# Branch A's output tiles: two gates taken from the buffers, and weights issued ahead of gates in SP's queue

## What is computed

```python
z = h @ p['w_in']
za, zb, zg = jnp.split(z, [A_COLS, A_COLS + B_COLS], axis=-1)
y_a, new_rwkv = _rwkv7_branch(za_mix, s_rwkv, p)
y_b, new_ret = _retention_branch(zb, s_ret, pos)
gates = jax.nn.sigmoid(zg.astype(jnp.float32)).reshape(bsz, t, 2, D_MODEL)
merged = (gates[:, :, 0] * (y_a.astype(h.dtype) @ p['w_branch_a'])
          + gates[:, :, 1] * (y_b.astype(h.dtype) @ p['w_branch_b']))
out = merged.astype(h.dtype) @ p['w_out']
```

## Time and profile before

| | |
|---|---|
| median of 3 runs | 4482.52 us (4481.86 to 4484.15) |
| profiled execution | 4492.62 us, span 4490.8 us |
| mean granted clock of TensorE | 0.958 of full speed |
| busy: PE, DVE, ACT, POOL | 94%, 44%, 31%, 6% of the span |
| DMA | 448.88 MB, mean 100 GB/s |
| loads of queries and keys, of values, of a head | 1280 KB each |
| weights of a branch A tile, a gate, a spilled tile | 512, 320, 320 KB |
| retention head 0 beside `ba`, first to last eviction | layer 0: 1252.3 to 1356.1 us, layer 1: 3498.1 to 3603.0 us |

### The profile page before, as it was taken

One profiled execution on the slowest core, in us unless ns is written; L12 is line 12 of the kernel. 1 busy time (PEld: TensorE's weight loads), 2 busy tenths in 40 slices (PEclk: granted clock), 3 DMA queues, 4 the chain that ended last, 5 costly groups with the idle time before them and its releaser, 6 DMA issues.

```text
span 4490.8 us, 87125 instructions
## 1 busy us (share of the span) xinstructions
PE 4208.0 (94%) x37680; PEld 3751.5 (84%) x37680; DVE 1955.1 (44%) x3032; ACT 1389.2 (31%) x2168; POOL 288.9 (6%) x464
## 2 busy tenths in 40 slices
PE   6999999999989987999989999999999899889997
PEld 5888899888866676999978888998888666789996
DVE  2444444434245543433354444444442455554444
ACT  3333333324223222322233333333242232232222
POOL 1000000000001111000100000000000011000000
PEclk7999999999989997999979999999999899989998
DMA  5122212212355565243421222122123465412221
GB/s 174 60 61 69 61 61 62 63 58 70 107 165 205 181 196 173 85 125 118 129 71 60 61 68 62 58 64 65 59 70 107 162 208 181 157 34 75 74 75 64
DMA packets 477320, 448.88 MB, mean 100 GB/s; under 512 B 18846, under 2 KB 409048, under 8 KB 476064
## 3 DMA queue, kind: packets, MB, share of 16 engines
q1 hardware_dynamic: 417712, 253.05, 18.6%
q0 software_dynamic: 41840, 157.01, 10.8%
q10 hardware_dynamic: 17408, 33.56, 2.0%
HBM read 345.79 MB, written 97.76 MB: 99 GB/s over the span
## 4 chain that ended last, share of the span: by engine, by line
PE 85%; DVE 7%; DMA 3%; ACT 3%; issue 2%; POOL 0%; ACTq 0%; DVEq 0%; SPq 0%; POOLq 0%
PE ps L731 83%; DVE scr L1915 2%; PE ps L735 1%; DMA w_raw<-in_w_branch_a_dram 1%; ACT scr L1372 1%; DMA scr<-in_ada_w_dram 1%; ACT w_hi L1385 1%; DVE acc L1915 1%; DVE h_lo L1915 1%; DVE w_lo L1928 1%; DVE scr L1917 1%; DVE lw L1915 1%; DMA w_raw<-in_w_out_dram 0%; ACT scr L1522 0%; DMA w_raw<-in_w_branch_b_dram 0%
## 5 line engine op out<-in xcount | busy, mean ns | idle before, releaser
L731 PE MATMUL ps<-h_hi,w_hi 128*128 128x320 f32 x4544 | 1105.1, 325 | 96.8 <-DVEq L1923 55.4
L731 PE MATMUL ps<-h_lo,w_hi 128*128 128x320 f32 x4544 | 1042.6, 311 | 0.0
L731 PE MATMUL ps<-h_hi,w_lo 128*128 128x320 f32 x4544 | 1041.6, 311 | 0.0
L731 PEld LDWEIGHTS ps<-h_hi,w_hi 128*128 128x128 f32 x4544 | 749.1, 190 | 185.1 <-issue 159.8
L731 PE MATMUL ps<-scr 64*64 64x64 f32 (+10 forms) x13248 | 809.5, 250 | 14.3 <-ACTq L1504 14.1
L731 PEld LDWEIGHTS ps<-scr 64*64 64x64 f32 (+4 forms) x13248 | 590.8, 141 | 212.6 <-issue 182.1
L731 PEld LDWEIGHTS ps<-h_lo,w_hi 128*128 128x128 f32 x4544 | 767.4, 190 | 0.0
L731 PEld LDWEIGHTS ps<-h_hi,w_lo 128*128 128x128 f32 x4544 | 766.3, 189 | 0.0
L1385 ACT ACTIVATE w_hi<-w_raw 128x1024 fp32r<-128x1024 f32 (+1 forms) x468 | 410.6, 878 | 797.7 <-PE ps L731 595.4
L1928 DVE TENSOR_TENSOR w_lo<-w_raw,w_hi 128x1024 fp32r<-128x1024 f32 (+1 forms) x468 | 469.4, 1003 | 364.0 <-ACT w_hi L1385 345.0
L1372 ACT ACTIVATE scr<-ps 128x512 f32<-128x512 f32 (+8 forms) x724 | 343.8, 475 | 780.4 <-PE ps L731 558.6
(11 more groups left out here) (151 smaller groups left out, 2946.2 us busy)
## 6 DMA issues: line engine op xcount, KB each, us to landing
w_raw<-in_w_in_dram SPq DMA_DIRECT2D x180, 512.0 KB, 3.8
scratch_z<-scr SPq DMA_DIRECT2D x128, 320.0 KB, 2.2
scr<-in_ada_w_dram POOLq DMA_DIRECT2D x40, 1024.0 KB, 6.1
scr<-in_state_ret_dram POOLq DMA_DIRECT2D x64, 512.0 KB, 4.8
out_dram<-scr ACTq DMA_DIRECT2D x64, 512.0 KB, 3.0
w_raw<-in_w_ffn_up_dram SPq DMA_DIRECT2D x64, 512.0 KB, 4.1
w_raw<-in_w_ffn_down_dram SPq DMA_DIRECT2D x128, 256.0 KB, 2.7
scr<-scratch_z POOLq DMA_DIRECT2D x24, 1280.0 KB, 9.0
```

Source lines behind the costliest of these rows:

```text
L731: return pe.matmul(out, lhsT, rhs, start=start, stop=stop, skip_group_check=True)
```

## The change

Spilled tiles are now 62 a layer (`STORED`): the last two, gates 6 and 7, stay in `ZT`. Branch A's tile i computes output tile (i + 6) % 8, so tiles 0 and 1 multiply with these two gates; their weights and their place in `ACC` move along. POOL's wait for `z_out` stands for 62 tiles and its two loads are gone, with the semaphore `gate_first`. Gates 0 to 5 are loaded by SP for tiles 2 to 7. In SP's queue the weights of tile i come first, behind the wait for the slot alone, and behind them the gate of tile i-1 with its wait for the eviction of tile i-3; at the last tile the gates of tiles 6 and 7 both.

```diff
+STORED = SPILLED - 2
             if name == "ba":
-                return ba_v[l, i]
+                return ba_v[l, (i + KD - 2) % KD]
...
                     if not isinstance(g, int) or g >= 2:
                         sp.wait_ge(lo_done, g - 1)
-                    if name == "ba" and i >= 2:
-                        sp.wait_ge(psum_read_v, freed(g - 1, "v"))
-                        sp.dma_start(ZT[:, i % 2], scratch["z"][GATE0 + i]).then_inc(gate_in[i % 2], 16)
                     sp.dma_start(WR[:, s, 0:kt], weight_of(l, name, i)).then_inc(w_in[s], 16)
+                    if name == "ba":
+                        for t in (i - 1, i) if i == KD - 1 else (i - 1,):
+                            if t >= 2:
+                                sp.wait_ge(psum_read_v, freed(START[l, "ba"] + t - 1, "v"))
+                                sp.dma_start(ZT[:, t % 2], scratch["z"][GATE0 + t - 2]).then_inc(gate_in[t % 2], 16)
...
-                        if kind == "own":
-                            spilled[g] = (l * SPILLED + i, i)
+                        if kind == "own" and i < STORED:
+                            spilled[g] = (i, i)
...
                 for i in range(2):
-                    po.wait_ge(z_out[i], 16 * (SPILLED // 2) * (l + 1))
-                    po.dma_start(ZT[:, i], scratch["z"][GATE0 + i]).then_inc(gate_first[i], 16)
+                    po.wait_ge(z_out[i], 16 * (STORED // 2) * (l + 1))
...
-                            f = l * SPILLED + o
+                            f = l * STORED + o
...
                             if i < 2:
-                                ve.wait_ge(gate_first[i], 16 * (l + 1))
+                                ve.wait_ge(psum_read_a, freed(START[l, "ba"], "a"))
                             else:
                                 ve.wait_ge(gate_in[i % 2], 16 * ((KD // 2 - 1) * l + i // 2))
-                            ve.tensor_tensor(halves(ACC[:, i]), two_banks(0), halves(ZT[:, i % 2]), MUL_).then_inc(psum_read_v, 1)
+                            ve.tensor_tensor(halves(ACC[:, (i + KD - 2) % KD]), two_banks(0), halves(ZT[:, i % 2]), MUL_).then_inc(psum_read_v, 1)
```

More of the change, by code:

```diff
@@ L402, in build @@
         stage_sem = {n: sem(n) for n in STAGES}
-        gate_first = [sem("gate_first0"), sem("gate_first1")]
         ya_hi, ya_lo, gate_in = sem("ya_hi"), sem("ya_lo"), [sem("gate_in0"), sem("gate_in1")]
```

## The result

| | before | after |
|---|---|---|
| median | 4483.34 us (4 runs, 4481.86 to 4484.44) | 4447.35 us (4 runs, 4442.24 to 4456.60) |
| profiled execution | 4492.62 us, span 4490.8 | 4442.60 us, span 4440.8 |
| ACT's waits for w_branch_a | 157.8 us, 12 waits | none |
| ba0 to ba7, layer 0 and 1 | 103.82 and 104.90 us | 88.54 and 87.21 us |

The ratio after to before is 0.9924, with a 95% interval of 0.9908 to 0.9941: 34 us of 4483, between 26 and 41. The forecast was 4446.7 us, a gain of 35.8.

A forecast was written before the change was run, and what follows sets the result against it. PE was taken as the bound, stalled behind ACT's waits for late branch A weights. Gains of 17.4 us in layer 0 and 18.4 in layer 1, other parts zero: 4482.5 - 35.8 = 4446.7 us, range 4438 to 4462.

The forecast's parts named there:

- The bound and the waits: Branch A beside head 0: ACT's twelve waits for weights, 157.8 us, all go; ba6's weights get about 23.5 us of lead.
- The control: Head 1's intervals, plus 3.53 us for 24 more matmuls, size head 0's: sum 75.6 us, gains 17.4 and 18.4 us.
- Interval 5 to 6: Head 0, between evictions of ba5 and ba6: forecast 13.4 us, between 12.75 and 16.28.
- The rival that DVE holds the tail: DVE's rotary pieces keep interval 5 to 6 at 18.25 and 17.39 us: gain falls 4.9 + 4.0, 4455.6 us; 12 in 100.
- Idle time and clock: Check on head 0's PE: 8.0 us idle plus 5.1 us clock, 13.1 a layer, 26 us as low end of the gain.
- Gates from the buffers: Gates 6 and 7 kept in ZT, POOL's states earlier: cost and gain zero, bound 0 to 1 us per layer.
- The gates' new place: Gates 2 to 7 behind weights in SP's queue, wanted 23 us or more later: zero; bb0's weights 0.5 us at most.
- The slower rival: A late gate, at gates 6 and 7, holds up eviction and PE: 4507 us if each lands at 28 us; 2 in 100.
- The time: Whole kernel: gain 35.8 us from 4482.5, giving 4446.7 us; 80 in 100 for 4440 to 4453.

The follow-up runs named there:

- run 7: Changed kernel with weights of branch A tile i held until the eviction of tile i-3: 4450.22 us, ratio 0.9936.
- run 11: Changed kernel with no DVE rotary piece between evictions 5 and 6 of a head, the first at point y1: 4445.58 us, ratio 0.9916.
- run 4: Changed kernel with the next head's first rotary piece on DVE moved ahead to point y1, later pieces one place forward: 4445.36 us, ratio 0.9908.
- Run 2: Changed kernel with SP's old queue put back, so only the new order of the tiles remains: 4469.46 us, ratio 0.9967.
- Run 6: Kernel before with POOL loading head 0's first three states and gates ahead of its two waits for spills: 4471.75 us, ratio 0.9982.
- run 1: Kernel before with SP's queue alone changed, branch A weights ahead of gates: 4451.87 us, ratio 0.9926.
- run 3: Changed kernel again, unaltered, for a second profile: 4449.29 us, ratio 0.9923.
- run 10: Changed kernel with each gate waiting for one eviction more, bb0's first weights behind them: 4459.68 us, ratio 0.9945.
- run 12: Kernel before again, unaltered, for a second profile: 4482.96 us in one execution.
- run 5: Changed kernel with weights of tile i waiting again for the eviction of tile i-2, gates still behind: 4467.56 us, ratio 0.9969.

## Why the prediction was right, point by point

**The bound and the waits.** Right. Twelve waits were forecast to go and twelve went. The lead is ample, though shorter than the 23.5 us of the prediction: ba6's weights left 20.2 us ahead of their split (1274.93 to 1295.18) and ba7's 20.5, since DVE splits ba4 and ba5 some 3 to 5 us into the interval and not at its start. Even one tile interval is enough (run 7).

**The control.** The steps for each interval held, bar one. Forecast and measured in layer 0: 11.83 and 11.82, 11.47 and 11.45, 11.99 and 11.99, 13.17 and 13.16, 13.4 and 14.49, 13.74 and 13.74 us; the sum 75.6 and 76.65. Head 1 of the same trace, plus 3.53 us for 24 more matmuls, gave three of the six to 0.02 us; 3 to 4 and 6 to 7 were taken as they stood in head 0, and stayed.

**Interval 5 to 6 was mis-sized by 1.1 us.** I had taken 13.4, "between 12.75 and 16.28 and nearest to the first". 13.17 is what PE sets (run 11); with DVE's two rotary pieces in it, it is 14.49. How much of that the larger split has was not separated. The rival that DVE holds the tail had the right engine for this interval, but a fraction of the size: 1.1 to 1.3 us, not 4 to 5, and in head 0 it did not lengthen the way to bb0 (runs 4 and 11): PE was busy through the whole interval, 14.49 of 14.49 us, so DVE's late eviction held nobody up.

**Idle time and clock.** The estimate from the other side, 13.1 us a layer, was 3 us short of the 93.02 - 76.65 = 16.4 us of layer 0. The missing part is idle time, not work "that overlapped badly". That estimate let head 0 keep the 3.5 us that PE stands idle in head 1's intervals. But head 1 has half the matmuls to fill them; in the changed kernel PE stood idle for 0.35 + 0.11 = 0.46 us in head 0's six. So 11.5 - 0.5 = 11.1 us of idle time went, and PE's busy time fell by the other 5.3 us, from 81.49 to 76.19, for which the estimate from the clock had 5.1. The clock did return to 1.00 in all six intervals. The rule of the Trainium skill (TensorE: Matmul & The Clock Gate, HAM oscillation) pointed the right way: by idle time alone a third of layer 0's gain would be missing. In layer 1 idle time fell by 10.4 us and busy time by 7.0, in all 17.4.

**Gates from the buffers: this step failed.** The prediction said "Cost and gain zero" of this part, for POOL's earlier states too: "PE had not waited for it, so zero again". Run 2 measured 12.7 us for it. PE had not waited for the states, but ba3's weights had, on the same DMA engines, and ACT, DVE and PE for those. I had asked who waits for the moved transfers and not what they travel beside. Run 6 puts their place in time down as the cause. The total does not suffer from it: with the weights ahead this gain is already in, because the eviction of a tile no longer holds back the weights, however long they take. The two parts share it and don't add: 12.7 us for the one, 30.3 for the other (run 1), 32.9 for both (run 3).

**The gates' new place.** Right in the change. The slower rival would have struck elsewhere than I had it: run 10 shows bb0's first weights, behind gate 7, as the first victim, at 10.4 us for one interval of delay.

**The time.** 35.8 us were forecast; the ratios of 0.9924 and 0.9923 say 34 to 35. The traces account for 33.0 and 32.6 us between ba0 and ba7 against the first profile of before, and for some 30 against run 12. The few us between these and the medians are within the scatter of executions and were not tracked down. The mechanism was right, but that 4446.7 came within 0.7 us of the median of 4447.35 is partly luck. Of the 35.8 us, 2.1 are missing in the changed kernel's intervals (76.65 and 76.64 for 75.6 twice), and 3.7 more hang on a profile of the kernel before whose intervals were longer than run 12's. The same kernel in run 3 had 4449.29 us.

## What to carry to other kernels

A queue that runs in order should hold what is wanted soonest and may leave soonest at its head; a wait for a buffer belongs behind the transfers that don't need that buffer. When an engine works through its program in order, one late load costs everything behind it, so look for another stretch of the same trace that does the same work without the wait, and read the size of the gain from it, interval by interval. And when a transfer moves, ask which others it used to travel beside: its own consumer may never have waited, and it can still be what made another one late.

## What the runs showed of the hardware

A load of 512 KB from SP's queue, issued behind one of 320 KB, landed in 4.4 us with POOL's queue idle (runs 2 and 6), in 10.0 us while 2.52 MB came through POOL's queue, and in 13.4 and 15.0 us beside the next head's queries, keys and values, in intervals in which POOL's queue moved 3.8 and 4.0 MB. With the waits gone the granted clock stood at 1.00 through 76.6 us of PE at 99% busy. In the kernel before, whose longest stops of PE in these intervals were 1.5 to 4.4 us in layer 0, it was 0.87 to 0.94 in three of the six.

Executions of one program fell into two groups by the place of the first branch A eviction, 1247 to 1248 or 1252 to 1253 us, in both the kernel before and the changed one. The difference is there at 74 us, in work that no edit touched, and it is the clock. In the first profile of the changed kernel PE did 94 matmuls from 58.8 to 69.3 us at a mean granted clock of 0.76, and it was 1.00 from 64.0 on. In run 3 the same matmuls took from 59.2 to 73.9 us, at 0.50 throughout. All profiles of the early group (the changed kernel's first, runs 2, 4, 5, 7 and 12) have 0.76 to 0.81 there; all others, the first of before among them, have 0.50. PE was busy nearly throughout in both groups (10.46 of 10.50 us and 14.62 of 14.70 in these two). Why the clock rises at 64 us in some executions and not before 74 us in others stays open.
